# Masks of the delta rule's score blocks applied late, one w_in evacuation and the cache transposes moved forward, seven more unread products per layer

## The reference

```python
for l in range(DEPTH):
    x = x + 0.5 * rmsnorm(swiglu(rmsnorm(x)), g)             # FFN a
    u = rmsnorm(x) @ w_in[l]                                 # 2688 columns, four head groups
    u_pool, u_rwkv, u_conv, u_sb = split(u)
    y_pool = grouped_linear(trailing_means(u_pool) - u_pool) # windows 2, 4, 8, 16
    y_rwkv = rwkv7(u_rwkv)                                   # delta rule, below
    y_conv = b * conv3(c * x_in)
    y_sb   = stick_breaking(q, concat(k_past, k), concat(v_past, v))
    x = x + rmsnorm(concat(y_pool, y_rwkv, y_conv, y_sb) @ w_out[l])
    x = x + 0.5 * rmsnorm(swiglu(rmsnorm(x)), g)             # FFN b

def step(S, inp):                                            # rwkv7, token by token
    s_kk = einsum('bhvk,bhk->bhv', S, kk_t)
    S = S * w_t - s_kk[..., None] * (kk_t * a_t) + v_t[..., None] * k_t
    return S, einsum('bhvk,bhk->bhv', S, r_t)
```

## Time and profile before

| | before |
|---|---|
| device time, median of 3 runs | 2706.59 us (2703.75 to 2709.93) |
| the profiled execution | 2707.43 us |
| its span, first to last instruction | 2705.5 us |
| TensorE busy | 2637.1 us (97%) |
| VectorE, ScalarE, GpSimd busy | 986.2, 753.6, 891.0 us |
| mean granted TensorE clock | 0.990 |

### The profile page before, as it was taken

The page is one execution under the profiler, slowest core; times in us unless marked ns, Lnnn a source line. Parts: engine busy times, 40 slices in busy tenths (PEclk is TensorE's granted clock), DMA queues, the critical chain, the costliest instruction groups (busy, mean ns, idle before and its releaser), DMA issues.

```text
span 2705.5 us, 48570 instructions
## 1 busy us (share of the span) xinstructions
PE 2637.1 (97%) x21066; PEld 2576.7 (95%) x21066; DVE 986.2 (36%) x1489; ACT 753.6 (28%) x1078; POOL 891.0 (33%) x440
## 2 busy tenths in 40 slices
PE   8999999999889999999999999999998999999998
PEld 8999999999789999999999999999987889999998
DVE  6222201775664422210252221028666663222103
ACT  4222211322523322221232222124134233222211
POOL 5333333432113433333353333325212143333331
PEclk9999999999999999999999999999998999999999
DMA  4222222322102222222222222222230013222222
GB/s 120 70 78 70 75 72 72 84 63 88 44 3 72 71 74 73 77 71 74 75 64 77 73 74 73 72 74 76 63 101 16 18 57 86 77 70 78 72 71 69
DMA packets 356052, 188.38 MB, mean 70 GB/s; under 512 B 16330, under 2 KB 354086, under 8 KB 355912
## 3 DMA queue, kind: packets, MB, share of 16 engines
q1 hardware_dynamic: 355668, 186.25, 23.9%
q10 hardware_dynamic: 244, 0.08, 0.0%
HBM read 179.50 MB, written 6.80 MB: 69 GB/s over the span
## 4 chain that ended last, share of the span: by engine, by line
PE 90%; DVE 5%; DVEq 2%; ACT 1%; issue 1%; DMA 1%; ACTq 0%; SPq 0%; POOL 0%
PE ps L1526 26%; PE ps L1528 26%; PE ps L1527 25%; PE ps L1572 3%; PE ps L1515 1%; DVE xT L1016 1%; PE ps L2025 1%; DVE h_split L1036 1%; PE ps L2041 1%; DVE ps L1012 1%; PE ps L2037 1%; PE ps L1722 1%; PE ps L1545 0%; PE ps L1520 0%; DVEq L1029 0%
## 5 line engine op out<-in xcount | busy, mean ns | idle before, releaser
L561 POOL TENSOR_TENSOR w_lo<-w_raw,w_hi 128x1024 fp32r<-128x1024 f32 (+1 forms) x330 | 781.7, 2370 | 1661.4 <-ACT w_hi L621 1660.3
L1526 PE MATMUL ps<-h_split,w_hi 128*128 128x384 f32 (+1 forms) x3520 | 1103.1, 313 | 5.7 <-DVE sb_qkv L1159 5.0
L1528 PE MATMUL ps<-h_split,w_lo 128*128 128x384 f32 (+1 forms) x3520 | 1092.5, 310 | 0.0
L1527 PE MATMUL ps<-h_split,w_hi 128*128 128x384 f32 (+1 forms) x3520 | 1082.3, 307 | 0.0
L1526 PEld LDWEIGHTS ps<-h_split,w_hi 128*128 128x128 f32 x3520 | 660.9, 188 | 11.5 <-DVE sb_qkv L1159 5.4
L1528 PEld LDWEIGHTS ps<-h_split,w_lo 128*128 128x128 f32 x3520 | 667.2, 190 | 0.0
L1527 PEld LDWEIGHTS ps<-h_split,w_hi 128*128 128x128 f32 x3520 | 662.6, 188 | 0.4
L621 ACT ACTIVATE w_hi<-w_raw 128x1024 fp32r<-128x1024 f32 (+1 forms) x330 | 342.3, 1038 | 811.2 <-DMA w_raw<-in_ffn_w_down 374.7
L1526 PE MATMUL ps<-hidden_split,w_hi 128*128 128x384 f32 (+1 forms) x1344 | 419.6, 312 | 0.0
L1098 DVE TENSOR_TENSOR scratch<-ps,square_sums 128x640 f32<-128x640 f32 x176 | 144.4, 824 | 752.5 <-PE ps L1528 749.9
L1528 PE MATMUL ps<-hidden_split,w_lo 128*128 128x384 f32 (+1 forms) x1344 | 416.6, 310 | 0.0
(11 more groups left out here) (320 smaller groups left out, 1977.8 us busy)
## 6 DMA issues: line engine op xcount, KB each, us to landing
w_raw<-in_ffn_w_gate SPq DMA_DIRECT2D x88, 512.0 KB, 3.8
w_raw<-in_ffn_w_up SPq DMA_DIRECT2D x88, 512.0 KB, 3.7
w_raw<-in_ffn_w_down SPq DMA_DIRECT2D x64, 448.0 KB, 3.5
w_raw<-in_w_in SPq DMA_DIRECT2D x42, 512.0 KB, 4.0
w_raw<-in_ffn_w_down SPq DMA_DIRECT2D x32, 512.0 KB, 3.7
w_raw<-in_w_out SPq DMA_DIRECT2D x16, 512.0 KB, 3.8
token_rows<-in_x_prompt SPq DMA_DIRECT2D x4, 512.0 KB, 5.5
k_cache<-in_cache_sb_k SPq DMA_DIRECT2D x2, 1024.0 KB, 5.7
```

Of the source, the lines that this page charges most:

```text
L561: nc.gpsimd.tensor_tensor(WLO[s][:, 0:n], RAW[s][:, 0:n], WHI[s][:, 0:n].bitcast(F32), ALU.subtract).then_inc(sem(f"lo_ready{s}"), 1)
L1526: MM(out, hi, mov[:, 0, cols], start=first, stop=False)
L1527: MM(out, hi, mov[:, 1, cols], start=False, stop=False)
L1528: return MM(out, lo, mov[:, 0, cols], start=False, stop=last)
```

## The change

It makes four edits.
1. `u_evac(16)` stands behind the first pooled chunk instead of behind both.
2. In a lane's slot VectorE goes from `LA` straight to `NT`, `XTR` and `X`. ScalarE copies `LR`, `KA` and `KR` unmasked from PSUM behind `TOK` and raises `scores_copied`. VectorE multiplies them by the masks in SBUF, for all lanes of the pair, at the T1 slot of level 0, and raises `scores_masked` there. TensorE's next lane and its first T1 wait for `scores_copied`; `scores_masked` is awaited where `KA` and `KR` are used.
3. `fill(k)` and `fill_out(k)` run at `it` = k (0 to 3).
4. `busy(3, 3)` stands before the second lane's scores of pair 1, `busy(3, 2)` before the first T1 of pairs 1 and 2, where pair 2 also waits for `yr_out` of the last prompt chunk.

```diff
@@ ScalarE
-                    if 1 <= it <= FILLS:
-                        fill_out(it - 1)
+                    if it < FILLS:
+                        fill_out(it)
@@ ScalarE, intra
                         A(TOK[:, t % 4], PS[:, 6:8, 0:G], ACT.Copy).then_inc(sem("rows_ready"), 1)
+                        beta, kappa = [PS[:, 4:6, w * G:(w + 1) * G].rearrange("p e (g a n) -> p e g a n", g=GC, a=2) for w in (0, 1)]
+                        act.wait_ge(sem("lt_ready"), l * TT + t + 1)
+                        A(by_lane(LR[:, t % 4]), beta[:, :, :, 1, :], ACT.Copy)
+                        A(by_lane(KA[:, a]), kappa[:, :, :, 0, :], ACT.Copy)
+                        A(by_lane(KR[:, t % 4]), kappa[:, :, :, 1, :], ACT.Copy)
+                        act.drain().then_inc(sem("scores_copied"), 1)
@@ VectorE, pooling
+                    if g == 0:
+                        u_evac(16)
                 fence().then_inc(sem("pool_in"), 1)
-                u_evac(16)
                 u_evac(17)
@@ VectorE, intra
-                        V.tensor_tensor(by_lane(LA[:, a]), beta[:, :, :, 0, :], tri[0], ALU.mult)
+                        V.tensor_tensor(by_lane(LA[:, a]), beta[:, :, :, 0, :], tri, ALU.mult)
                         fence().then_inc(sem("lt_ready"), 1)
-                        V.tensor_tensor(by_lane(LR[:, slot]), beta[:, :, :, 1, :], tri[1], ALU.mult)
-                        V.tensor_tensor(by_lane(KA[:, a]), kappa[:, :, :, 0, :], tri[0], ALU.mult)
-                        V.tensor_tensor(by_lane(KR[:, slot]), kappa[:, :, :, 1, :], tri[1], ALU.mult)
-                        fence().then_inc(sem("scores_masked"), 1)
                         V.tensor_tensor(NT[:, 0, a], LA[:, a], every_head(LEV[:, 1, :]), ALU.mult)
...
                     v, update = divmod(k - len(lanes), 2)
+                    if not update and v == 0:
+                        for a, t in lanes:
+                            dve.wait_ge(sem("scores_copied"), l * TT + t + 1)
+                            before, upto = [every_head(TRI[:, (0 if t < PT else 2) + w, :]) for w in (0, 1)]
+                            V.tensor_tensor(KA[:, a], KA[:, a], before, ALU.mult)
+                            V.tensor_tensor(LR[:, t % 4], LR[:, t % 4], upto, ALU.mult)
+                            V.tensor_tensor(KR[:, t % 4], KR[:, t % 4], upto, ALU.mult)
+                            fence().then_inc(sem("scores_masked"), 1)
@@ TensorE
-                    if 1 <= it <= FILLS:
-                        fill(it - 1)
+                    if it < FILLS:
+                        fill(it)
@@ TensorE, scores
-                        pe.wait_ge(sem("scores_masked"), q)
+                        if p:
+                            busy(3, 3)
+                        pe.wait_ge(sem("scores_copied"), q)
                         pe.wait_ge(sem("rows_ready"), q)
@@ TensorE, intra
-                            pe.wait_ge(sem("scores_masked"), l * TT + lanes[-1][1] + 1)
+                            if p == 2:
+                                pe.wait_ge(sem("yr_out"), l * (CHUNKS + 1) + NCH * 2)
+                            if p:
+                                busy(3, 2)
+                            pe.wait_ge(sem("scores_copied"), l * TT + lanes[-1][1] + 1)
...
+                            pe.wait_ge(sem("scores_masked"), l * TT + t + 1)
```

More of the change, by code:

```diff
@@ L1392, in intra @@
                         q, slot = l * TT + t, t % 4
-                        tri = [TRI[:, (0 if t < PT else 2) + w, :].unsqueeze(1).unsqueeze(1).broadcast_to([P, 2, GC, CH]) for w in (0, 1)]
-                        beta, kappa = [PS[:, 4:6, w * G:(w + 1) * G].rearrange("p e (g a n) -> p e g a n", g=GC, a=2) for w in (0, 1)]
+                        tri = TRI[:, 0 if t < PT else 2, :].unsqueeze(1).unsqueeze(1).broadcast_to([P, 2, GC, CH])
+                        beta = PS[:, 4:6, 0:G].rearrange("p e (g a n) -> p e g a n", g=GC, a=2)
                         dve.wait_ge(sem("scores_in"), q + 1)
@@ L2003, in kappa_values @@
                     pe.wait_ge(sem("state_rhs_out"), nth(l, "state_rhs_out"))
+                    pe.wait_ge(sem("scores_masked"), (l + 1) * TT)
                     for c in (0, 1):
```

## The result

The changed kernel takes 2717.55 us (median of 13 runs, 2705.94 to 2722.27) against 2706.59 us (13 runs, 2703.43 to 2709.93): ratio 1.0037 with a 95% interval of [1.0027, 1.0046]. That is slower, and outside the range of 2696 to 2713. Not only the median moved: the runs of before lie within 6.5 us, those of after within 16.3 us. The profiled execution took 2721.24 us, 3.7 us above the median.

The account below looks back on a forecast made before the run. TensorE, busy for 97% of the span, was taken as the bound. From the profiled 2707.43 us: evacuation -3.15, fills -2.1, attention clock -1.9, score blocks +4.0, clock falls +1.6 gave 2705.9 us; range 2696 to 2713.

Parts of the forecast that it names:

- Evacuation and fills: Tile 18 of w_in starts earlier, -3.15 us; attention units lose the fill wait, -2.1, and a low-clock spell, -1.9.
- Score blocks: Delta rule: VectorE's NT and late masks wait for GpSimd; pairs +2.1, +0.8, -0.9 us per layer, +4.0 in all.
- Rival 1: Delta rule: VectorE wins the ties and GpSimd waits, so blocks miss the path; 2692.3 us, up to 2700; chance 0.28.
- Unread products: Pairs 1 and 2: seven products of 0.50 us per layer lie in existing TensorE waits, costed at nothing.
- The clock: Falls at pair 0 (chance 0.3), pair 1 (0.2) and tile 18's wait (0.12), 1.31 us each, two layers: +1.6 us.
- Rival 2: Late masks open waits in pairs 0 and 1 that drop the clock in both layers; 2713.0 us, slower; chance 0.17.

Follow-up runs that it names:

- e1: The kernel before with only the evacuation between the chunks and the earlier cache fills; 2698.43 us, -7.4 us beside before.
- e4: The change without its seven unread products per layer; 2705.69 us, -0.2 us beside before.
- e5: The change without the two unread products ahead of pair 2's first T1, pair 1's five kept; 2705.10 us, -0.9 us beside before.
- e3: The change without late masks: evacuation, fills and unread products added to the kernel before; 2696.88 us, -9.0 us beside before.
- e7: The change with the late masks made by GpSimd behind its own NT, in place of VectorE; 2700.03 us, -6.0 us beside before.
- e6: The change with eight more unread products per layer, in pair 2's waits for the state; 2708.53 us, +2.5 us beside before.

## Why the prediction was wrong

- **Evacuation and fills**: right. Forecast -3.15 - 2.1 - 1.9 = -7.2 us, measured -7.4 (e1). The agreement in size is in part luck, since the fall in pair 1 that e1's profile lacks was not in the sum.
- **Score blocks**: right in mechanism and size. Both blocks fell on VectorE, and pair 0 lost 2.03 us (2.1). Without the saving of 1.5 us per layer that I had put on the unread products the term was +4.0 + 3.0 = +7.0 us; measured, e4 less e1, +7.3 us. That agreement is in part luck: e4's profile has a fall of 6.8 us in the levels of layer 1, which the term doesn't hold. Rival 1, that VectorE wins the ties, is out. The Trainium skill ("SBUF — State Buffer", "Summary: rules for kernel authors") has the second to issue fully blocked until the first finishes, when VectorE has two SBUF inputs and GpSimd reads SBUF; the rows agree in both directions (1.54 us on VectorE behind GpSimd, 1.49 us on GpSimd behind a mask).
- **Unread products**: here it failed. I costed them at nothing, with 1.5 us per layer saved behind pair 2's first T1. The saving is in the rows (2.06 instead of 3.4 us), but the term is +11.1 us (the change less e4), not -3.0. In pair 2, where I had -0.9 us per layer, the profile has +7.2 and +2.2 us.
- **The clock**: the step that let this through. I listed falls at three waits, each at 1.31 us, the price of a fall of some 3 us, and took pair 2's fall as removed. I didn't ask what the clock would do at the next thin place once it had not fallen at the first. In pair 2's levels I priced the delay of the state update (-0.4 to -2.4) as time, not as thinner work for TensorE. The fall there lasted 6.8 to 20.5 us.
- **Rival 2** (the clock pays, 2713.0 us) had the right sign and cause but the wrong places: pair 0 did fall in layer 0 (3.41 us), pair 1 in neither layer, and most of the loss came from pair 2, which it didn't name.

What stays open: why the fall in the levels lasts 20 us in layer 0 and 7 us in layer 1, and how often it comes. Two profiles of the change have it in both layers, but its fastest runs (2705.94 and 2707.85 us) lie where e4 and e5 lie, so they may lack it. The mean granted clock of the runs points the same way: 0.994 and 0.993 in these two, 0.987 to 0.991 in the eleven others. A difference of 0.005 in the mean clock over 2715 us is 27 us at the lower level (an estimate from these numbers), as long as the profile's two falls together (20.47 and 6.82 us). No profile of such a run is there to show it.

## What to carry to other kernels

A fall of the clock that is filled with unread work can come back at the next thin place, and there it may last longer; look at the waits behind it, not only at the one that is filled. When an operand moves from PSUM to SBUF on VectorE, look at what GpSimd starts at the same moment: a common semaphore makes a tie on every pass, and a later wait on GpSimd's side removes it when its result has slack. Test edits in pairs: the unread products cost nothing without the late masks (e3 against e1) and 11.1 us with them.

## What the runs showed of the hardware

- One semaphore released both `NT`: GpSimd started 0.01 us ahead in every pair of both layers (722.06 against 722.07), and VectorE waited. It waited too where it started 0.01 us ahead (before, layer 1, L1302: 2.96 us from 1972.98, beside GpSimd's 2.40 from 1972.99; undisturbed 0.75). A GpSimd run of back-to-back instructions held up four VectorE instructions in a row (e7).
- One fall of the clock lasted 20.47 us, with TensorE busy for 19.84 us of it. Ahead of it TensorE had waited 0.83 and 0.99 us within 2.93 us. With unread products in the first of the two waits (e6) the next 20 us stayed at 1.00.
